# Spread weight conversion over two token groups, and re-stage the sample caches, in a two-layer hybrid encoder on eight cores

## The reference

```python
for l in range(2):
    x = x + 0.5 * (silu(rms(x)@w1_gate[l]) * (rms(x)@w1_up[l])) @ w1_down[l]      # D 1024, hidden 2816
    qa, ka, va, qb, kb, vb = split(rms(x) @ w_in[l], 6)                           # 512 columns each
    # group A: 8 heads x 64, QK-norm, own chunk of 64 frames and the 8 chunks before, relative bias
    # group B: 4 heads, q/k halves of 64, values of 128, QK-norm, rotary: softmax(1) - lam * softmax(2)
    x = x + concat(A, B) @ w_out[l]
    x = x + 0.5 * (silu(rms(x)@w2_gate[l]) * (rms(x)@w2_up[l])) @ w2_down[l]
```

## Time and profile before

| | us |
|---|---|
| median of 3 runs | 8012.99 |
| the 3 runs | 8454.6, 8012.99, 7601.93 |
| the profiled execution, its own time | 7586.13 |
| its span on the slowest core | 7585.1 (the cores: 7554.7 to 7585.1) |
| TensorE / VectorE / ScalarE / GpSimd busy in the span | 6630.0 / 2912.0 / 2651.3 / 1403.3 |
| mean granted TensorE clock of this core | 0.960 |
| HBM read / written | 973.12 MB / 149.95 MB |

### The profile page before, as it was taken

The page is one execution under the profiler, slowest core; times in us unless marked ns, Lnnn a source line. Parts: engine busy times, 40 slices in busy tenths (PEclk is TensorE's granted clock), DMA queues, the critical chain, the costliest instruction groups (busy, mean ns, idle before and its releaser), DMA issues.

```text
span 7585.1 us, 114887 instructions; the slowest of 8 cores (7554.7 to 7585.1 us)
## 1 busy us (share of the span) xinstructions
PE 6630.0 (87%) x39776; PEld 3525.2 (46%) x39776; DVE 2912.0 (38%) x5057; ACT 2651.3 (35%) x4204; POOL 1403.3 (19%) x1750
## 2 busy tenths in 40 slices
PE   5777788989899998989898989899999989896777
PEld 2333334454444445454444454544444454555666
DVE  4545534343333343333434343433343433433332
ACT  1412315151524335261414152524333351614343
POOL 1112111202111121212121212121121212122121
PEclk9899999999999999999999999999999999998888
DMA  8699762424233342424242424243343424256666
GB/s 264 216 310 306 224 206 85 146 86 157 97 121 122 115 154 69 147 73 160 97 146 98 158 89 142 95 148 116 109 134 103 148 70 149 77 181 213 208 222 200
DMA packets 452258, 1130.56 MB, mean 149 GB/s; under 512 B 38384, under 2 KB 166128, under 8 KB 451696
## 3 DMA queue, kind: packets, MB, share of 16 engines
q1 hardware_dynamic: 433568, 1059.23, 43.5%
q0 software_dynamic: 18128, 63.97, 2.2%
HBM read 973.12 MB, written 149.95 MB: 148 GB/s over the span
## 4 chain that ended last, share of the span: by engine, by line
PE 61%; DVE 11%; ACT 10%; issue 7%; DMA 5%; POOL 4%; SPq 2%; DVEq 0%; ACTq 0%; POOLq 0%
PE psb L542 14%; PE psb L522 12%; PE psb L518 11%; PE psb L756 5%; POOL tC L533 4%; PE psb L889 3%; PE psb L986 3%; PE psb L1007 3%; DVE tA L528 2%; PE psb L696 2%; ACT tA L531 2%; ACT eT L1065 2%; SPq L270 1%; PE psb L1166 1%; ACT tq L759 1%
## 5 line engine op out<-in xcount | busy, mean ns | idle before, releaser
L533 POOL TENSOR_TENSOR tC<-tA,rstdT 128x512 f32<-128x512 f32 (+1 forms) x792 | 954.4, 1205 | 4198.5 <-ACT tA L531 4081.0
L522 PE MATMUL psb<-hT,wring 128*128 128x512 bf16 (+1 forms) x6336 | 1430.9, 369 | 132.3 <-DVE BIG L536 126.6
L518 PE MATMUL psb<-hT,wring 128*128 128x512 bf16 (+1 forms) x6336 | 1434.5, 369 | 87.2 <-DVE tA L528 78.6
L542 PE MATMUL psb<-BIG,wring 128*128 128x512 bf16 (+1 forms) x6336 | 1322.5, 370 | 43.8 <-DVE wring L412 38.6
L531 ACT ACTIVATE tA<-tA 128x512 f32<-128x512 f32 (+1 forms) x792 | 479.8, 606 | 2218.3 <-DVE tA L528 2217.9
L536 DVE TENSOR_TENSOR BIG<-psb,tC 128x512 bf16<-128x512 f32 (+1 forms) x792 | 524.2, 662 | 1757.8 <-POOL tC L533 1757.8
L522 PEld LDWEIGHTS psb<-hT,wring 128*128 128x128 bf16 x6336 | 588.1, 98 | 895.0 <-issue 355.3
L518 PEld LDWEIGHTS psb<-hT,wring 128*128 128x128 bf16 x6336 | 618.9, 98 | 785.6 <-issue 133.4
L542 PEld LDWEIGHTS psb<-BIG,wring 128*128 128x128 bf16 x6336 | 621.1, 98 | 735.4 <-issue 76.9
L528 DVE TENSOR_TENSOR tA<-psb,rstdT 128x512 f32<-128x512 f32 (+1 forms) x792 | 515.7, 651 | 164.7 <-ACT rstdT L485 164.6
L994 ACT ACTIVATE eT<-psb 128x1024 bf16<-128x1024 f32 (+2 forms) x640 | 532.7, 892 | 106.4 <-PE psb L986 57.5
(11 more groups left out here) (179 smaller groups left out, 6233.0 us busy)
## 6 DMA issues: line engine op xcount, KB each, us to landing
wring<-wsc SPq DMA_DIRECT2D x1280, 512.0 KB, 3.9
wsc<-wring SPq DMA_DIRECT2D x160, 512.0 KB, 9.4
vb<-w_gate SPq DMA_DIRECT2D x66, 512.0 KB, 9.7
vb<-w_up SPq DMA_DIRECT2D x66, 512.0 KB, 10.7
vb<-w_down SPq DMA_DIRECT2D x66, 512.0 KB, 12.3
vb<-cbk SPq DMA_DIRECT2D x64, 512.0 KB, 5.1
vb<-cbv SPq DMA_DIRECT2D x64, 512.0 KB, 4.5
vb<-w_in SPq DMA_DIRECT2D x36, 512.0 KB, 11.6
```

The lines of the kernel that those rows point to most:

```text
L518: P.add("pe", lambda kc=kc, bg=bg, wg=wg, fl=fl: nc.tensor.matmul(psb[bg][:, 0:T], wg[:, kc, fl * 128:(fl + 1) * 128], hT[:, kc, 0:T], sta ...
L522: P.add("pe", lambda kc=kc, bu=bu, wu=wu, fl=fl: nc.tensor.matmul(psb[bu][:, 0:T], wu[:, kc, fl * 128:(fl + 1) * 128], hT[:, kc, 0:T], sta ...
L533: P.add("pool", lambda ts=ts: nc.gpsimd.tensor_tensor(out=tC[ts][:, 0:T], in0=tA[ts][:, 0:T], in1=rstdT[:, 0:T], op=ALU.mult), [("t", ts, ...
L542: P.add("pe", lambda: nc.tensor.matmul(psb[ab][:, 0:T], wd[:, fl, dcl * 128:(dcl + 1) * 128], aT[:, fc, 0:T], start=(fc == 0), stop=(fc == ...
```

## The change

What it does:

- **Weights over two groups.** A first conversion pass now runs through groups 0 and 1 (`NCONV = 2 * NW`). In group 0 every tile is still loaded as float32 and cast; only tiles of w_in and w_out and FFN tiles of even `idx` are written to `wsc`. In group 1 those are fetched as bf16, and the FFN tiles of odd `idx` (64 of 168 tiles) are loaded as float32 and cast again, and written. From group 2 on all are fetched.
- **Staging of weights.** Twelve parts instead of eight in group 0 (four more in the upper halves of `kbT`, each of which takes two DMAs of 256 KB), eight in group 1.
- **Casts.** A tile's first half stays on VectorE, its second goes to GpSimd for w_in and w_out and to ScalarE for FFN tiles.
- **FFN banks.** Chunk `fc` uses banks 2 (fc mod 4) and the next: all eight banks.
- **Prompt attention.** In group B `o_transpose` is put off by 4 tiles where i is 0 and by 6 otherwise, in bank 4 where that is more than nk // 2, else in bank 6; the last ones come after the sixth unit of group A, in bank 7. In group A `o_transpose(0, hp - 1)` is written ahead of the division.
- **Sample caches.** Six staging buffers instead of three. `piece_dma` is also called in the projection stage, after each of the last eight w_in tiles, until six pieces are under way. Key pieces are first cast to bf16 (into rows 1 to 6 of `hT`, GpSimd and VectorE in turn, one piece ahead), then transposed in bf16 and copied from bf16 PSUM. Value pieces are copied by GpSimd and VectorE in turn, ScalarE no more. The ones are set once, for layer 1. The last four matmuls of a stream are written at the fourth unit of the next stream.

```diff
+    NCONV = 2 * NW
+        for p_ in range(2):
+            parts[("k", l_, p_)] = ([kbT[l_][:, 2 * p_ + a_, 1024:2048].bitcast(F32) for a_ in range(2)],
+                                    [("kbx", l_, p_)])
+    late = [k_ for k_ in parts if k_[0] == "k" or (k_[0] == "v" and k_[2] > 0)]
+    early = late + [k_ for k_ in parts if k_ not in late]
...
+    def written_first(tid):
+        (l, name, idx) = cat_list[tid][0]
+        return name in ("in", "out") or idx % 2 == 0
+
+    def converts(n):
+        return n < NW or (n < NCONV and not written_first(n % NW))
+
+    def writes_back(n):
+        return written_first(n % NW) if n < NW else converts(n)
...
     def first_cast(n):
...
-            P.add("dve", lambda buf=buf, hf=hf: nc.vector.tensor_copy(
-                out=wring[:, s, hf * 1024:(hf + 1) * 1024], in_=buf), toks, [("w", s)])
+                if hf == 0:
+                    P.add("dve", lambda: nc.vector.tensor_copy(out=dst, in_=buf), tk, [("w", s)])
+                elif name in ("in", "out"):
+                    P.add("pool", lambda: nc.gpsimd.tensor_copy(out=dst, in_=buf), tk, [("w", s)])
+                else:
+                    P.add("act", lambda: nc.scalar.copy(out=dst, in_=buf), tk, [("w", s)])
...
     def first_pass(n):
+        while fp["load"] < min(n + LOOK + 3, NCONV):
+            cast_to(min(fp["load"] - 3, n + LOOK + 1))
+            if converts(fp["load"]):
+                first_load(fp["load"])
             fp["load"] += 1
+        cast_to(n + LOOK + 1)
+        while fp["back"] < min(n + LOOK, NCONV):
+            if writes_back(fp["back"]):
+                first_back(fp["back"])
             fp["back"] += 1
+        while fp["fetch"] < min(n + LOOK + 1, NCONV):
+            if not converts(fp["fetch"]):
+                fetch(fp["fetch"])
+            fp["fetch"] += 1
...
-                bg, bu = rot(), rot()
+                bg = 2 * (fc % 4)
+                bu = bg + 1
...
-                    deferred.append([idx + min(nk // 2, 6), o_transpose, (1, h)])
+                    lag = 4 if i == 0 else 6
+                    deferred.append([idx + lag, o_transpose, (1, h, 6 if lag <= nk // 2 else 4)])
...
+            if u == 3 and hp > 0:
+                o_transpose(0, hp - 1, 6)
             if u % 2 == 1:
...
-            if u == 3 and hp > 0:
-                o_transpose(0, hp - 1)
...
+        def piece_cast():
...
+                if isK:
+                    kb_ = 1 + pstate["kb"] % 6
...
+                    cast(hT[:, kb_, :], cstg[sl][:, k, :], CT[sl], [("hT", kb_)])
                 else:
...
-                    put_v(("pool", "dve", "act")[vc[0] % 3], vfull, nh, cstg[sl][:, k, :], CT[sl], tok)
+                    put_v(("pool", "dve")[vc[0] % 2], vfull, nh, cstg[sl][:, k, :], CT[sl], tok,
+                          l == 1 and s_ == 0 and isBc)
+
+        def piece_conv():
...
+            for _ in range(NCS):
+                piece_dma()
+            while pstate["cast"] < min(n + 2, len(pieces)):
+                piece_cast()
...
+                pv = psb[b][:, 0:256].bitcast(BF16)
+                for c in range(4):
+                    P.add("pe", lambda c=c: nc.tensor.transpose(
+                        pv[:, c * 128:(c + 1) * 128], hT[:, kb_, c * 128:(c + 1) * 128], identb[:]),
+                        [("hT", kb_), "c"], [PS(b)])
```

253 lines of the change are left out of this document (153 added, 100 removed).

## The result

The changed kernel is faster by 2.75%: ratio 0.9725, 95% interval 0.9696 to 0.9753. Its median is 7390.47 us of 4 executions (lowest 7381.41); the profiled one took 7388.71 us with a span of 7387.7 (its slowest core is core 5), against 7586.13 and 7585.1 before (core 0).

What follows compares the result with a forecast made beforehand. Group 0's FFN was taken as held by the DMA engines, later prompt groups' FFN by TensorE, the sample group by neither. 7586 - 85 + 8 - 52 - 40 - 22 - 95 = 7300 us, range 7190 to 7440.

Steps and rivals of the forecast that it cites:

- B: Group 1: reading odd FFN tiles again as float32 fits beside TensorE's work; costs 8 us, bounds 0 and 40.
- A: Group 0: writing back about half the FFN weights saves DMA time; gain 85 us, bounds 50 to 105.
- E: Sample FFN: eight banks remove the recurring bank waits; gain 22 us, bounds 8 to 30.
- F: Sample attention: six staging slots and bf16 transposes leave DMA longest, 146 us a stage; gain 95 us for both stages.
- D: Prompt attention: moved output transposes wait less for VectorE; gain 40 us, bounds 10 and 60.
- R3: Rival, groups 0 and 1: ScalarE's weight casts block the SiLU queue, making the kernel slower, 7620 us; chance 0.05.
- C: Prompt FFN: rotation over all eight banks removes up-projection bank waits; gain 52 us, bounds 30 to 60.
- R1: Rival: group 0 does not get faster and group 1 pays 28 us instead of 8; 7405 us; chance 0.12.
- R2: Rival, sample attention: six slots do not keep the DMA busy, stage keeps 184 us; 7375 us; chance 0.16.

Runs made afterwards that it cites:

- run 1: Changed kernel without the spreading: every weight tile written back in group 0 and fetched as bf16 in group 1; 7351 us (core span).
- Run 8: run 7's three edits on the changed kernel, but with every tile written back in group 0 and fetched in group 1; 7312 us.
- run 7: Changed kernel with bf16 fetches issued before loads and write-backs, write-backs one tile later, and the FFN up multiply taken late; 7252 us.
- run 11: Changed kernel with all weight casts on VectorE, as before the change; 7413 us.
- run 3: Changed kernel with each bf16 fetch issued ahead of the float32 load and write-back in SP's queue; 7372 us.
- run 4: Changed kernel with VectorE taking each FFN chunk's up multiply after the next chunk's gate bank; 7270 us.
- run 5: Changed kernel with fetch first and up multiply late together; 7471 us at a low clock, group 1 gate/up 332 us by the medians.
- runs 2: Changed kernel with the FFN's four-bank rotation of before; 7447 us.
- run 12: Changed kernel with the output transposes of prompt attention as before the change; 7438 us (core span).
- run 9: Changed kernel with three cache staging slots instead of six; 7473 us.

## Why the prediction was right or wrong

The direction, the place of the largest gain and the range were right (7390 lies inside 7190 to 7440); the size was not. The gain forecast against the profiled execution, 286 us, is 1.45 times the 197 measured. The miss of 88 us by steps: B +64, A +28, E +20, other stages +7, less F 20 and D 11 that came out better. That the misses of F and D lie on the other side is luck: without them the gain would have been 166.

- **A, write-backs of group 0: -85 forecast, -57 measured** (group 0 without attention: FFN 36, projection 14, the rest 6). The step that failed is that group 0's FFN is held by the DMA engines, so that dropped bytes are dropped time down to TensorE's 119 us. It is so while everything is written: run 1, with the casts already split, shows share 1.01 and nearly the old length in the first row below, and its group 0 without attention is only 6 us shorter than before. But once the bytes were dropped the next limit was reached at once: TensorE's waits for casts, 95 us in group 0, in a chain in which each engine stands in order. Run 8 against run 7 shows 74 us for the same bytes once that chain is shortened, and in run 7 the stage is back at share 0.98 (second row), now at 86 us. The prediction took the split of the casts as costing nothing and bringing nothing; it brings 45 us (run 11), 15 of them in the projection stages, which I had passed over because they keep their bytes.

```profile
366.00:467.00 101.00, 82.35 (x349) 35.05 (x354) 41.50 (x72) 36.77 (x52) 25.31 (x20) 0.95 1.01 315
```
```profile
351.00:437.00 86.00, 78.39 (x349) 34.68 (x355) 43.27 (x71) 36.97 (x52) 24.95 (x20) 0.98 0.98 291
```

- **B, second float32 reading: +8 forecast, +72 measured** (group 1's FFN; run 1 gives 81). This is the step that decided. The capacity sum was right: a gate/up stage's 0.72 of 98 us is 71 us of DMA where 69 was forecast, and with the queues mended the share is 0.83 (0.87 forecast). The sign named for a mis-sized B came: gate/up stages of group 1 at 85 us or more, here 95 to 101. What failed is the sentence "behind at most a load and a write-back": the fetch also stands behind the *wait* of that write-back, for a cast on ScalarE, behind one on VectorE, behind the previous chunk's chain. I had written such a wait in line down as R3, but for SiLUs held by casts; it ran the other way round, casts held by the SiLU chain, and cost 67/64 = 1.0 us per tile of group 1, where R3 needed 1.4 over the tiles of both groups. By the medians of group 1, the order of SP's queue alone is worth 20 us (run 3), the late multiply alone 29 (run 4), both together 51 (run 5), and the later write-backs nothing more (run 7, 50). Some 30 us of the spreading's cost stay even then (run 7 against run 8). TensorE still waits 20 us for fetches there, and these take 6.3 us to land against 4.1, which points to the DMA load at a share of 0.83; no run separated it from what is left of the order.
- **C, eight banks: -52 forecast, -52 in groups 2 to 7** (gate/up -92, down +40). The number held with a wrong sentence inside, and so by luck: "VectorE then has a backlog of four chunks, at 1.4 us each against 3.5 us of TensorE: it catches up." Busy time is not the period of a serial chain. The chain takes 3.52 us a chunk, so the backlog is carried into the down stage; runs 2 and 4 show its 39 us from both sides. The gate/up stages gained 92, more than the 56.9 of the earlier trace rows. In the kernel before, L536 comes every 3.52 us from its second chunk to its last, so the chain paced TensorE (3.46) all along. By an estimate from these two figures that is 0.06 us in each of 528 chunks, 32 us, in gaps too short to be prominent among the waits.
- **D, prompt transposes: -40 forecast, -51 measured, -58 by run 12.** L1006 (L960 before) now waits 25 us for VectorE where the forecast left about 40. The half that I took back for exponentials came back only in small part: the wait of L1032 (L986 before) for them rose from 108.1 to 127.8 us in the whole run, and that of L1127 (L1080) fell from 73.7 to 59.5. These 51 us are of the attention stages alone; by the medians of the cores they shrink by 47, and the w_out stages behind them grow by 8, so that the net gain is near the 40 forecast.
- **E, sample FFN: -22 forecast, -2 measured.** The same failed sentence as in C, and here it is the whole term: the chain is 2.24 us a chunk, before and after the change, against 1.8 of TensorE, so eight banks only move the wait into the down stage (-18 and +16). With the chain mended (run 4) the FFN falls by a further 27 us, and fetches become what TensorE waits for, as I had expected one step too early.
- **F, sample attention: -95 forecast, -115 measured.** The DMA bound was the right one: share 0.91, 134 and 138 us where 146 was forecast. A bf16 transpose costs 0.102 us in the changed kernel's first stage (29.3 us of TensorE for 288; 0.111 forecast). Most of what was over-careful is the 15 us for what is not overlapped. The sentence that no row shows GpSimd and VectorE blocking each other was a misreading: the earlier trace rows has a mean of 0.694 us for GpSimd's cast, and in the same kernel one takes 0.61 alone and 0.86 beside VectorE's (last section).

Of the rivals, R1 (group 0 no faster) and R2 (slots don't keep the DMA busy) fell, R2 clearly: run 9 shows what it would have looked like. R3 in its own words fell too: without ScalarE's casts group 0 is 45 us longer, not shorter (run 11). What it has in common with what took the missing time is engines in order that pass a late landing or cast on to work that does not need it. Its sign, ScalarE's waits for weight landings beside waits in TensorE's FFN rows, was there in group 0:

```profile
ACT wring L442 <- DMA vb<-w_down: 57.1, 14, 7.8
```

So the sign did not tell the held SiLU from the late cast; only run 11 did.

## What to carry to other kernels

Before moving bytes between stages, look not only at whether the receiving stage's DMA share has room but what each in-order queue does between two transfers: a prefetch written behind a store inherits the store's wait for its producer, and the producer's place in its own engine's order. And compare the period of the serial chain through several engines (here 3.52 us), not each engine's busy time (1.4), with the consumer's period: more buffers in front of a chain that is as slow as the consumer move its wait to the next stage; one reordered instruction removed it.

## What the runs showed of the hardware that was not expected

GpSimd's casts get slower beside VectorE's. A row block of a cache, 128x512, is copied from float32 to bf16 within SBUF by either engine. GpSimd's copies before and after the change (duration min/median/max in ns, first and last start):

```profile
L644 POOL CAST vb<-vb x42: 609/610/864, 6891.5 to 7470.3; 128x512 bf16<-128x512 f32 x42
```
```profile
L1210 POOL CAST hT<-vb x40: 604/808/870, 6803.1 to 7275.9; 128x512 bf16<-128x512 f32 x40
```

The two lengths, near 610 and near 865, can be told apart in the timeline. First two casts of GpSimd in the kernel before, one beside VectorE's and one alone, then a pair of the changed kernel in which GpSimd started first:

```profile
6905.98 0.43 DVE L646 CAST vb<-vb 128x512 bf16<-128x512 f32 x1 [0.66 <-DMA vb<-cbv]
6906.02 0.86 POOL L644 CAST vb<-vb 128x512 bf16<-128x512 f32 x1 [9.12 <-DMA vb<-cbv]
...
6909.65 0.61 POOL L644 CAST vb<-vb 128x512 bf16<-128x512 f32 x1
```
```profile
6883.76 0.61 POOL L1210 CAST hT<-kbT 128x512 bf16<-128x512 f32 x1 [2.42 <-PE psb L1255]
6883.85 0.80 DVE L1212 CAST hT<-vb 128x512 bf16<-128x512 f32 x1
```

The one that starts first takes its usual time, 0.43 us on VectorE and 0.61 on GpSimd; the one that starts up to 0.1 us behind it takes 0.2 to 0.4 us more. In the kernel before, the 12 GpSimd casts of this kind that began 0.03 us behind such a VectorE cast took 862 to 864 ns, and the 37 that met less than 0.08 us of one took 609 to 612. In the changed kernel most of them meet one (95 of 160 casts of this shape, L684 among them, take over 0.7 us).

The prediction quoted the Trainium skill's page "SBUF — State Buffer", section "SBUF: two separate sides": the two engines exclude each other at a shared port pair, and the one that starts first keeps it. The traces agree on who waits. The wait is less than the whole of the other's instruction: GpSimd's cast loses 0.25 us to one of 0.43. It did not decide here, as the DMA share was 0.91 in the stage and GpSimd was busy 57 of its 134 us.
